# Values of two attentions computed token-major by their projections, instead of projected and then transposed

## The chip, the core and the metric

One core of a Trainium2 chip runs the whole program in one launch. The metric is the device time of that core in microseconds (us), the median of repeated runs. Nothing else runs on the chip.

## What is computed

Two transformer blocks run one after the other on 512 tokens of width 1024, in float32. The change lies in the first block, between its input norm and its attentions. Cut to that:

```python
h = rmsnorm(x, norm_mix_g)                       # (512, 1024)
q_a, k_a, v_a, q_b, k_b, v_b, gl_a, gl_b = jnp.split(h @ w_in, SPLITS, axis=-1)
# v_a: (512, 768), 12 heads of 64, in three groups of 4 with dilations 1, 4 and 16
# v_b: (512, 512), 8 heads of 64
o_a = dilated_attention(q_a, k_a, v_a)           # per group: softmax over every d-th key, probabilities @ v_a
o_b = stick_breaking_attention(q_b, k_b, v_b)    # probabilities @ v_b
merged = sigmoid(gl_a + b_a) * (o_a @ w_up_dil) + sigmoid(gl_b + b_b) * (o_b @ w_up_sb)
x = x + merged @ w_out
```

## The kernel before

**Products.** Activations lie feature-major: a tile holds 128 features on its partitions and the 512 tokens along it. A *slab* is 128 output features. For each slab TensorE (PE) takes the 8 tiles of 128 input features one after the other, loads a 128x128 block of the weight matrix as the stationary operand and streams the 512 tokens past it. Numbers are split into a high and a low part in the matmul's own format (`wh`, `wl` for weights, `Ah`, `Al` for activations), so that each product is three: high by high, high by low, low by high. A slab is therefore 8 x 3 = 24 matmuls 512 wide, into one PSUM bank; banks 0 and 1 alternate. This is `products`, called by `full_slab` (L2327 is the matmul in it).

**Weights.** Loads of 1 MB (256 columns of the matrix, all 1024 rows) go to `raw`, two slots; each serves two slabs. Per slab ScalarE (ACT) writes `wh` (L895) and VectorE (DVE) `wl` (L1439), both double-buffered. `lo_ready` counts them for PE.

**Order.** The slabs have numbers: 0 to 17 are q, k and v of the dilated attention (`T_QKV_A`), 18 to 25 the first gates, 26 to 37 q, k and v of the stick-breaking attention (`T_QKV_B`), 38 to 45 the second gates. The dilated attention itself is woven in behind slabs 18 to 29, the stick-breaking one behind slabs 38 and later. `slab_done` counts slabs that PE finished, `evac_done` slabs that DVE took out of PSUM; a slab starts when the one two before it is evacuated (`slab_start`).

**Values before.** Slabs 12 to 17 and 34 to 37 are values. The attentions need them token-major (tokens on the partitions), as the stationary operand of "probabilities times values". So each value slab is computed feature-major, evacuated by DVE into `vt` or `vtb` (L1915, L1484: times `RS`, the norm's reciprocal root of each token along the row), turned by PE in four 128x128 transposes (`v_turn`, L2578) into bank 6 or 7, and copied by ACT to `Vna` or `Vnb` (`v_copy`, L1180). For the heads with dilation 4 and 16 the evacuation writes the tokens sorted by their residue modulo 4 (`by_class`), so that the four transposes give one residue each:

```python
def by_class(ap):
    return ap.rearrange("p (c i) -> p i c", c=4)
```

**The start.** The input is turned to feature-major by PE (`turn_x`, L2494, four transposes for each of the 8 feature tiles), ACT takes out the high part (`x_hi`, L1149) and a plain copy (`x_copy`, L1145), DVE the low part (`x_lo`, L1846), and POOL and DVE split the first weights (L711, L1852). PE works on slabs 0 and 1 piece by piece as these arrive: `first_hh(k)`, `first_lh(k)` and `first_hl(k)` are the three products of feature tile k, each for both slabs (L2517). `warm(n)` (L2509) multiplies the identity by itself n times into a bank that nobody reads.

Of the kernel before, what the change touches and what calls it, by code (L numbers as in the profile page):

```python
# [171 lines left out]
def build(nc, d):  # L172
# [21 lines left out]
    with ctx:  # L194
# [59 lines left out]
        vt = region(13568, 2, 512)  # L254
# [9 lines left out]
        vtb = region(14080, 2, 512)  # L264
# [43 lines left out]
        r_x = stat[:, 4, 8:12]  # L308
# [24 lines left out]
        vtrans_done, vnat_copied = sem("vtrans_done"), sem("vnat_copied")  # L333
# [190 lines left out]

        def raw_slab(t):
            p, half, kt, n = slab[t]
            return raw_half(p % 2, half, kt, n)
# [76 lines left out]
        def _(sp):  # L604
# [50 lines left out]
            sp.wait_ge(vnat_copied, 6)  # L655
# [224 lines left out]
        def _(act):  # L880
# [280 lines left out]
            x_copy(5)  # L1161
            x_hi(6)
            x_hi(7)
            x_copy(7)
# [13 lines left out]
            def v_copy(i, dst):  # L1178
                act.wait_ge(vtrans_done, i + 1)
                act.activation(dst, ps[:, 6 + i % 2, :].rearrange("p (a b) -> p a b", a=4), ACT.Copy)\  # L1180
                   .then_inc(vnat_copied, 1)

            for t in range(T_QKV_A + 3, T_GATE_A):
                convert(t + 1)
                if t == T_QKV_A + 9:
                    act.wait_ge(vec_ready, 1)
                    act.activation(halfb[:, :], vecT[:, B_GATE:B_GATE + 16], ACT.Copy, scale=0.5)\
                       .then_inc(halfb_ready, 1)
                if t >= T_QKV_A + 14:
                    v_copy(t - 14, Vna[:, :, (t - 14) * P:(t - 13) * P])  # L1190
            v_copy(4, Vna[:, :, 4 * P:5 * P])
            convert(T_GATE_A + 1)
            v_copy(5, Vna[:, :, 5 * P:6 * P])
# [50 lines left out]
            for t in range(T_GATE_A + DIL_STEPS, T_GATE_B):  # L1244
                convert(t + 1)
                i = t - T_QKV_B - 8 - 2
                if i >= 0:
                    v_copy(6 + i, Vnb[:, :, i * P:(i + 1) * P])
            act.preload_act_table(ACT.Sigmoid)
            for i in (2, 3):  # L1250
                v_copy(6 + i, Vnb[:, :, i * P:(i + 1) * P])
# [176 lines left out]
        def _(dve):  # L1428
# [443 lines left out]
            def qkv_a(t, src):  # L1872

                i = t - T_QKV_A
                if i >= 14:
                    dve.wait_ge(vtrans_done, i - 13)
                dst = qa[:, i, :] if i < 6 else ka[:, i - 6, :] if i < 12 else vt[:, i % 2, :]
                if i < 6:
                    return by_block(dst), src.rearrange("p (n r c) -> p n r c", n=4, c=4)
                if i in (6, 7, 12, 13):  # L1880
                    return dst, src
# [29 lines left out]

            for t in range(T_QKV_A + 3, T_GATE_A + 1):
                dve.wait_ge(slab_done, t)
                dst, src = qkv_a(t - 1, dense_psum(t - 1, ONE))
                dve.tensor_tensor(dst, src, qkv_a(t - 1, RS[:, 0:S1])[1], ALU.mult).then_inc(evac_done, 1)  # L1915
# [38 lines left out]
            def qkv_b(t):  # L1954
                i = t - T_QKV_B
                if i == 0:
                    dve.wait_ge(scores_done, 8)
                if i >= 10:
                    dve.wait_ge(vtrans_done, 6 + i - 9)
                scaled(t, qb[:, i, :] if i < 4 else kb[:, i - 4, :] if i < 8 else vtb[:, i % 2, :], ONE)  # L1960
# [349 lines left out]
        def _(pe):  # L2310
# [20 lines left out]
            def slab_start(t):  # L2331
                pe.wait_ge(lo_ready, t + 1)
                if t >= 2:
                    pe.wait_ge(evac_done, t - 1)

# [207 lines left out]
            warm(4)  # L2543
            first_hh(0)
            first_hh(1)
            first_lh(0)
            turn_x(2)
            turn_x(3)
            first_lh(1)
            first_hl(0)  # L2550
# [66 lines left out]
            def dil_turn(u):  # L2617
                n, jp, nb, w, c1 = dil_unit(u)
                lg = Lg[u % 2]
                pe.wait_ge(p_norm, 2 * u + 2)  # L2620
                if u >= 1:
# [13 lines left out]
            def dil_pv(u):  # L2635
                n, jp, nb, w, c1 = dil_unit(u)
                pe.wait_ge(pt_copied, u + 1)
                if u == 0:
                    pe.wait_ge(vnat_copied, 6)
# [30 lines left out]
            for u in range(DIL_STEPS):  # L2670
                full_slab(T_GATE_A + u, Ah, Al, 0, ONE)
                if u == 0:
                    pe.wait_ge(evac_done, T_GATE_A)
                    v_turn(5, vt[:, 1, :])
# [8 lines left out]
            for t in range(T_GATE_A + DIL_STEPS, T_GATE_B):  # L2683
                full_slab(t, Ah, Al, 0, ONE)
                i = t - T_QKV_B - 9
                if i >= 0:
# [20 lines left out]
            def sb_turn(w):  # L2707
                n, hp, nk = sb_unit(w)
                pe.wait_ge(sb_probs, w + 1)
                if w >= 1:  # L2710
# [7 lines left out]
            def sb_pv_mm(w):  # L2718
                n, hp, nk = sb_unit(w)
                pe.wait_ge(sb_pt_copied, w + 1)  # L2720
                if w == 0:
                    pe.wait_ge(vnat_copied, 10)
# [10 lines left out]
            for i in range(SB_STEPS):  # L2733
                if i < 16:
# [6 lines left out]
                    if i == 0:  # L2741
                        pe.wait_ge(evac_done, T_GATE_B)
                        v_turn(9, vtb[:, 1, :])
# [198 lines left out]
```

## Time and profile before

| what | value |
|---|---|
| median of 3 runs | 1410.69 us (1410.23 to 1412.68) |
| the profiled execution | 1411.16 us, of which the span shown is 1409.4 us |
| granted TensorE clock, mean over the span | 0.999 |
| PE busy | 1402.3 us of the span, 8550 matmuls |
| DVE busy | 917.2 us |
| ACT busy | 592.8 us |
| POOL busy | 212.3 us |

The profile is of one execution; its time lies 0.5 us above the median. Busy time of PE counts overlapping matmuls once and their ends are modelled, so how long a stretch of matmuls really takes is read from the chain that ended last, which gives starts and counts.

### The profile page before, as it was taken

To read this page: it belongs to the slowest core of one execution; us is meant where nothing else is said; L and a number is where in the kernel's file an instruction comes from. 1 tells how busy PE (TensorE), PEld (TensorE's weight loads), DVE (VectorE), ACT (ScalarE), POOL (GpSimd) and SP (SyncE) were. 2 spreads that over 40 slices of the span, in tenths; PEclk is the share of its full clock that TensorE was granted. 3 is DMA by queue.
4 is the path that set the end of the run, shared out by engine and by line. 5 is a ranking of instruction groups with operands and counts; after the bars stand their busy time and mean duration, and the time that the engine had idled before them with its cause. 6 is when DMAs were issued, how large, how long until landed. Compare 5 with 4: busy or idle time off the path is not lost.

```text
span 1409.4 us, 21396 instructions
## 1 busy us (share of the span) xinstructions
PE 1402.3 (99%) x8550; PEld 1178.4 (84%) x8550; DVE 917.2 (65%) x1229; ACT 592.8 (42%) x844; POOL 212.3 (15%) x215
## 2 busy tenths in 40 slices
PE   9999999999999999999999999999999999999998
PEld 7887778777888989989888997778888998989886
DVE  6535433665757858677656677656756967758775
ACT  5124531554434435343244435344444535344353
POOL 5000000000022302211423020000022221302310
PEclk9999999999999999999999999999999999999999
DMA  5223113201227845736222322132225673937563
GB/s 183 90 90 113 61 60 96 84 31 60 90 90 179 181 125 152 169 106 162 90 90 85 110 61 84 60 105 90 90 90 135 178 166 109 215 93 184 144 174 110
DMA packets 154858, 161.58 MB, mean 115 GB/s; under 512 B 4010, under 2 KB 144660, under 8 KB 154788
## 3 DMA queue, kind: packets, MB, share of 16 engines
q1 hardware_dynamic: 122868, 129.12, 28.6%
q0 software_dynamic: 31904, 31.46, 12.3%
q8 instruction: 51, 0.84, 0.3%
q14 instruction: 19, 0.16, 0.0%
q10 hardware_dynamic: 16, 0.00, 0.0%
HBM read 157.68 MB, written 2.10 MB: 113 GB/s over the span
## 4 chain that ended last, share of the span: by engine, by line
PE 99%; DMA 0%; ACT 0%; DVE 0%; issue 0%; ACTq 0%
PE ps L2327 67%; PE ps L2374 17%; PE ps L2323 4%; PE ps L2447 3%; PE ps L2701 1%; PE ps L2517 1%; PE ps L2728 1%; PE ps L2714 1%; PE ps L2821 1%; PE ps L2605 0%; PE ps L2494 0%; PE ps L2578 0%; PE ps L2646 0%; PE ps L2625 0%; DMA arena<-in_x 0%; PE ps L2903 0%
## 5 line engine op out<-in xcount | busy, mean ns | idle before, releaser
L2327 PE MATMUL ps<-AA,wh 128*128 128x512 f32 x1600 | 504.2, 397 | 0.0
L2327 PEld LDWEIGHTS ps<-AA,wh 128*128 128x128 f32 x1600 | 297.0, 188 | 69.3 <-DVE wl L1439 0.8
L2327 PE MATMUL ps<-BB,wh 128*128 128x512 f32 x1088 | 342.2, 396 | 0.2 <-issue 0.2
L2327 PE MATMUL ps<-AA,wl 128*128 128x512 f32 x800 | 315.0, 394 | 0.0
L895 ACT ACTIVATE wh<-raw 128x1024 fp32r<-128x1024 f32 (+2 forms) x149 | 141.5, 950 | 253.7 <-PE ps L2327 243.8
L2327 PEld LDWEIGHTS ps<-BB,wh 128*128 128x128 f32 x1088 | 202.2, 188 | 49.3 <-issue 1.6
L2327 PE MATMUL ps<-BB,wl 128*128 128x512 f32 x544 | 214.0, 393 | 0.0
L1439 DVE TENSOR_TENSOR wl<-raw,wh 128x1024 fp32r<-128x1024 f32 (+2 forms) x149 | 169.9, 1140 | 47.8 <-ACT wh L895 47.5
L2327 PEld LDWEIGHTS ps<-AA,wl 128*128 128x128 f32 x800 | 150.5, 188 | 34.4
L2327 PEld LDWEIGHTS ps<-BB,wl 128*128 128x128 f32 x544 | 102.3, 188 | 23.3
L2374 PE MATMUL ps<-Hl,wh 128*128 128x256 f32 x384 | 108.0, 281 | 0.0
L1484 DVE TENSOR_TENSOR arena<-ps,RS 128x512 f32<-128x512 f32 (+2 forms) x59 | 40.7, 690 | 87.0 <-PE ps L2327 83.1
L1516 DVE TENSOR_TENSOR wl<-raw,wh 128x1024 fp32r<-128x1024 f32 x48 | 62.3, 1297 | 31.0 <-ACT wh L943 15.9
L2374 PE MATMUL ps<-Hl,Sh 128*128 128x256 f32 x288 | 81.1, 282 | 0.0
L2374 PEld LDWEIGHTS ps<-Hl,wh 128*128 128x128 f32 x384 | 72.3, 188 | 0.0
L943 ACT ACTIVATE wh<-raw 128x1024 fp32r<-128x1024 f32 x36 | 38.1, 1060 | 63.5 <-PE ps L2327 63.5
L1578 DVE SCALAR_TENSOR_TENSOR zf<-ps,RS 128x512 f32<-128x512 f32 x48 | 33.2, 692 | 45.2 <-PE ps L2327 44.4
L2374 PEld LDWEIGHTS ps<-Hl,Sh 128*128 128x128 f32 x288 | 54.2, 188 | 0.2
L2374 PE MATMUL ps<-AA,wh 128*128 128x256 f32 x192 | 54.3, 283 | 0.0
L2374 PE MATMUL ps<-BB,wh 128*128 128x256 f32 x192 | 54.0, 281 | 0.0
L2374 PE MATMUL ps<-AA,wl 128*128 128x256 f32 x192 | 53.8, 280 | 0.0
L2374 PE MATMUL ps<-BB,wl 128*128 128x256 f32 x192 | 53.8, 280 | 0.0
(397 smaller groups left out, 2231.2 us busy)
## 6 DMA issues: line engine op xcount, KB each, us to landing
raw<-in_w_in SPq DMA_DIRECT2D x38, 1024.0 KB, 5.2
raw<-in_w_ff SPq DMA_DIRECT2D x31, 1024.0 KB, 5.5
raw<-in_w_mlp_in SPq DMA_DIRECT2D x16, 1024.0 KB, 5.4
raw<-in_w_mlp_out SPq DMA_DIRECT2D x16, 1024.0 KB, 4.9
zf<-in_w_mlp_out POOLq DMA_DIRECT2D x48, 256.0 KB, 4.6
zf<-in_w_ff POOLq DMA_DIRECT2D x48, 256.0 KB, 4.8
raw<-in_w_out SPq DMA_DIRECT2D x8, 1024.0 KB, 4.9
arena<-in_x SPq DMA_DIRECT2D x4, 512.0 KB, 6.9
```

The costliest lines, as they stand in the source:

```text
L895: act.activation(w_slab(wh, t % 2, kt), raw_slab(t), ACT.Copy).then_inc(hi_ready, 1)
L943: act.activation(w_slab(wh, j % 2, KT), raw_half((p0 + i) % 2, j % 2, KT, 2), ACT.Copy)\
L1439: dve.tensor_tensor(w_slab(wl, t % 2, kt), raw_slab(t), w_slab(wh, t % 2, kt), ALU.subtract)\
L1484: dve.tensor_tensor(tokens(dst, kind), dense_psum(t, kind)[0:rows], tokens(scale, kind), ALU.mult)\
L1516: dve.tensor_tensor(w_slab(wl, slot, KT), raw_half(p % 2, slot, KT, 2), w_slab(wh, slot, KT), ALU.subtract).then_inc(lo_ready, 1)
L1578: dve.scalar_tensor_tensor(out=f, in0=halves(dense_psum(t0 + j, which)), scalar=0.0, in1=halves(RS[:, 0:S1]), op0=ALU.max, op1=ALU.mult).t ...
L2323: last = pe.matmul(dense_psum(t_ps, ALL)[:, half, :], a[:, k, :], b[:, o0 + k, half * HALF2:(half + 1) * HALF2], start=start, stop=stop)
L2327: last = pe.matmul(dense_psum(t_ps, kind), a[:, k, :], b[:, o0 + k, col0:col0 + S1], start=start, stop=stop)
L2374: mm = pe.matmul(ps[:, bank, 0:HB], w[:, k, :], hidden_part(x, k, b), start=(first and k == 0 and i == 0), stop=(k == 3 and i == 2), skip_ ...
L2447: mm = pe.matmul(ps[:, bank, :], x, v[:, k, :], start=(first and k == 0 and n == 0), stop=(k == 3 and n == 2), skip_group_check=True)
L2517: return pe.matmul(dense_psum(t, ONE), w_slab(w, t, KT)[:, k, :], x[:, k, 0:S1], start=first, stop=last)
L2701: pe.matmul(ps[:, 2 + b, 0:nk], qb[rows, hp, n * P:(n + 1) * P], kb[rows, hp, 0:nk], start=True, stop=False)
```

## The change

Value slabs are computed in pairs, token-major. The stationary operand becomes a 128x128 block of the activations (128 features by 128 tokens), the moving one a block of the weights, 128 features by 256 output columns, which is two slabs at once. Both halves of a pair keep their slab number: the first takes input tiles 0 to 3, the second tiles 4 to 7 (`value_unit`), each 4 x 4 x 3 = 48 matmuls 256 wide, into two banks of 4 to 7 that hold 4 token blocks by 256 columns. For the heads with dilation 4 and 16 (slabs 14 to 17) the stationary block is every fourth column of `Ah` or `Al`, so that the residues come out sorted. DVE evacuates a pair in four TENSOR_SCALARs of 256 columns, times the reciprocal root of the token, which now lies on the partition (`r_x`; for sorted tokens `r_class`, got by four transposes of `RS` into bank 6 and a copy of four columns). `vt`, `vtb`, `v_turn`, `v_copy` and their semaphores go; the waits that stood on `vnat_copied` now stand on `evac_done`. At the start `warm(4)` goes, `first_hl(0)` moves ahead of the turns of tiles 2 and 3, and ACT does `x_copy(5)` behind `x_hi(7)`.

```diff
@@ -522,8 +520,25 @@
             r, c = (CHUNKS - 1) * DM + (0 if upper else S1), 0 if left else S1
             return w[r:r + S1, c:c + S1]
 
+        T_V_A, T_V_B = T_QKV_A + 12, T_QKV_B + 8
+        V_ENDS = {T_V_A: T_GATE_A, T_V_B: T_GATE_B}
+
+        def value_start(t):
+
+            return next((v for v, end in V_ENDS.items() if v <= t < end), None)
+
+        def value_banks(t):
+
+            return 4 + 2 * ((t - value_start(t)) // 2 % 2)
+
+        def value_blocks(w, t):
+
+            return w[:, t % 2, :].rearrange("p (k n) -> p k n", k=4)
+
         def raw_slab(t):
             p, half, kt, n = slab[t]
+            if value_start(t) is not None:
+                return raw[:, p % 2, half * DM:(half + 1) * DM].rearrange("p (k n) -> p k n", k=KT)
             return raw_half(p % 2, half, kt, n)
 
         def lr_slab(col):
...
@@ -1158,9 +1173,9 @@
             x_hi(5)
             x_copy(3)
             x_copy(4)
-            x_copy(5)
             x_hi(6)
             x_hi(7)
+            x_copy(5)
             x_copy(7)
             for a in range(4):
                 if a == 1:
...
@@ -1175,22 +1190,13 @@
             act.activation(r_x, r_x, ACT.Sqrt).then_inc(sqrt_ready, 1)
 
 
-            def v_copy(i, dst):
-                act.wait_ge(vtrans_done, i + 1)
-                act.activation(dst, ps[:, 6 + i % 2, :].rearrange("p (a b) -> p a b", a=4), ACT.Copy)\
-                   .then_inc(vnat_copied, 1)
-
             for t in range(T_QKV_A + 3, T_GATE_A):
                 convert(t + 1)
                 if t == T_QKV_A + 9:
                     act.wait_ge(vec_ready, 1)
                     act.activation(halfb[:, :], vecT[:, B_GATE:B_GATE + 16], ACT.Copy, scale=0.5)\
                        .then_inc(halfb_ready, 1)
-                if t >= T_QKV_A + 14:
-                    v_copy(t - 14, Vna[:, :, (t - 14) * P:(t - 13) * P])
-            v_copy(4, Vna[:, :, 4 * P:5 * P])
             convert(T_GATE_A + 1)
-            v_copy(5, Vna[:, :, 5 * P:6 * P])
 
             act.wait_ge(halfb_ready, 1)
 
...
@@ -1909,10 +1908,27 @@
                 q, r = qkv_a(t, RS[:, 0:S1])
                 dve.tensor_tensor(q, q, r, ALU.mult).then_inc(late_scaled, 1)
 
+            def value_rows(dst, t, r):
+                dve.wait_ge(slab_done, t + 1)
+                at = (t - value_start(t)) // 2 * 256
+                for a in range(4):
+                    mul = dve.tensor_scalar(dst[:, a, at:at + 256],
+                                            ps[:, value_banks(t) + a // 2, a % 2 * 256:a % 2 * 256 + 256],
+                                            r[:, a:a + 1], None, ALU.mult)
+                    if a % 2:
+                        mul.then_inc(evac_done, 1)
+
             for t in range(T_QKV_A + 3, T_GATE_A + 1):
-                dve.wait_ge(slab_done, t)
-                dst, src = qkv_a(t - 1, dense_psum(t - 1, ONE))
-                dve.tensor_tensor(dst, src, qkv_a(t - 1, RS[:, 0:S1])[1], ALU.mult).then_inc(evac_done, 1)
+                if t - 1 < T_V_A:
+                    dve.wait_ge(slab_done, t)
+                    dst, src = qkv_a(t - 1, dense_psum(t - 1, ONE))
+                    dve.tensor_tensor(dst, src, qkv_a(t - 1, RS[:, 0:S1])[1], ALU.mult).then_inc(evac_done, 1)
+                elif (t - 1 - T_V_A) % 2:
+                    value_rows(Vna, t - 1, r_x if t - 1 < T_V_A + 2 else r_class)
+                if t == T_V_A:
+                    dve.wait_ge(r_turned, 1)
+                    dve.tensor_copy(r_class, ps[:, 6, 0:S1:P]).then_inc(r_class_ready, 1)
+                    dve.wait_ge(r_class_ready, 1)
                 if t < T_GATE_A:
                     convert(t + 1)
                 if t in (T_QKV_A + 4, T_QKV_A + 5):
...
@@ -2330,8 +2347,26 @@
 
             def slab_start(t):
                 pe.wait_ge(lo_ready, t + 1)
-                if t >= 2:
+                if t in (T_GATE_A, T_GATE_A + 1):
+                    pe.wait_ge(evac_done, T_V_A)
+                elif t in (T_GATE_B, T_GATE_B + 1):
+                    pe.wait_ge(evac_done, T_V_B)
+                elif t >= 2:
                     pe.wait_ge(evac_done, t - 1)
+
+            def value_unit(t, by_residue):
+                pe.wait_ge(lo_ready, t + 1)
+                half = (t - value_start(t)) % 2
+                h, l = value_blocks(wh, t), value_blocks(wl, t)
+                for k in range(4):
+                    for a in range(4):
+                        of = slice(a, S1, 4) if by_residue else slice(a * P, (a + 1) * P)
+                        xh, xl = Ah[:, 4 * half + k, of], Al[:, 4 * half + k, of]
+                        for i, (x, w) in enumerate(((xh, h), (xh, l), (xl, h))):
+                            mm = pe.matmul(ps[:, value_banks(t) + a // 2, a % 2 * 256:a % 2 * 256 + 256], x, w[:, k, :],
+                                           start=(half == 0 and k == 0 and i == 0 and a % 2 == 0),
+                                           stop=(half == 1 and k == 3 and i == 2), skip_group_check=True)
+                mm.then_inc(slab_done, 1)
 
             def full_slab(t, Oh, Ol, o0, kind, ready=None, col0=0):
                 kt = slab[t][2]
...
@@ -2540,14 +2575,13 @@
 
             turn_x(0)
             turn_x(1)
-            warm(4)
             first_hh(0)
             first_hh(1)
             first_lh(0)
+            first_hl(0)
             turn_x(2)
             turn_x(3)
             first_lh(1)
-            first_hl(0)
             first_hl(1)
             first_hh(2)
             turn_x(4)
...
@@ -2570,14 +2604,6 @@
                 mm.then_inc(slab_done, 1)
 
 
-            def v_turn(i, src):
-
-                if i >= 2:
-                    pe.wait_ge(vnat_copied, i - 1)
-                for a in range(4):
-                    mm = pe.transpose(ps[:, 6 + i % 2, a * P:(a + 1) * P], src[:, a * P:(a + 1) * P], ident[:, :])
-                mm.then_inc(vtrans_done, 1)
-
             for t in range(2, T_GATE_A):
                 if t == 3:
                     def first_stats():
...
@@ -2585,15 +2611,23 @@
                         pe.wait_ge(xt_copied_act, len(X_ON_ACT))
                         stats(0)
                     slab_with_stats(t, (Ah, Al), ONE, None, first_stats, 2)
+                elif t < T_V_A:
+                    full_slab(t, Ah, Al, 0, ONE)
                 else:
-                    full_slab(t, Ah, Al, 0, ONE)
+                    if t == T_V_A:
+                        pe.wait_ge(meta_copied, 1)
+                    if t == T_V_A + 2:
+                        pe.wait_ge(r_class_ready, 1)
+                    if t == T_V_A + 4:
+                        pe.wait_ge(evac_done, T_V_A + 2)
+                    value_unit(t, t >= T_V_A + 2)
                 if t == 3:
                     turn_vectors()
-                if t >= 13:
-                    pe.wait_ge(evac_done, t)
-                    if t == 13:
-                        pe.wait_ge(x_diag, 5)
-                    v_turn(t - 13, vt[:, (t - 1) % 2, :])
+                if t == T_V_A - 2:
+                    pe.wait_ge(x_diag, 5)
+                    for c in range(4):
+                        mm = pe.transpose(ps[:, 6, c * P:(c + 1) * P], RS[:, c:S1:4], ident[:, :])
+                    mm.then_inc(r_turned, 1)
 
 
             def dil_scores(u):
...
@@ -2681,13 +2714,14 @@
 
 
             for t in range(T_GATE_A + DIL_STEPS, T_GATE_B):
-                full_slab(t, Ah, Al, 0, ONE)
-                i = t - T_QKV_B - 9
-                if i >= 0:
-                    pe.wait_ge(evac_done, t)
-                    if i == 0:
-                        pe.wait_ge(oa_ready, 4)
-                    v_turn(6 + i, vtb[:, i % 2, :])
+                if t < T_V_B:
+                    full_slab(t, Ah, Al, 0, ONE)
+                    continue
+                if t == T_V_B:
+                    pe.wait_ge(pt_copied, 8)
+                if t == T_V_B + 2:
+                    pe.wait_ge(oa_ready, 4)
+                value_unit(t, False)
 
 
             def sb_scores_mm(w):
```

How it moves instructions, at the places that the prediction speaks of. First PE at the start of the program, before (L2494 turns `xnat`, the input as it lies in memory, in `arena`; L2509 is `warm`, L2517 the pieces of slabs 0 and 1):

```order
4 L2494 MATMUL ps<-ident,arena 128x128 [waits x_in0]
5 L2494 MATMUL ps<-ident,arena 128x128 x3
6 L2494 MATMUL ps<-ident,arena 128x128 [waits x_in0]
7 L2494 MATMUL ps<-ident,arena 128x128 x3
8 L2509 MATMUL ps<-ident 128x128 x4
9 L2517 MATMUL ps<-AA,wh 128x512 [waits hi_split,w_first_hi]
10 L2517 MATMUL ps<-AA,wh 128x512
11 L2517 MATMUL ps<-AA,wh 128x512 [waits hi_split,w_first_hi]
12 L2517 MATMUL ps<-AA,wh 128x512
13 L2517 MATMUL ps<-AA,wh 128x512 [waits act_ready]
14 L2517 MATMUL ps<-AA,wh 128x512
15 L2494 MATMUL ps<-ident,arena 128x128 [waits x_in1]
```

and now:

```order
4 L2529 MATMUL ps<-ident,arena 128x128 [waits x_in0]
5 L2529 MATMUL ps<-ident,arena 128x128 x3
6 L2529 MATMUL ps<-ident,arena 128x128 [waits x_in0]
7 L2529 MATMUL ps<-ident,arena 128x128 x3
8 L2552 MATMUL ps<-AA,wh 128x512 [waits hi_split,w_first_hi]
9 L2552 MATMUL ps<-AA,wh 128x512
10 L2552 MATMUL ps<-AA,wh 128x512 [waits hi_split,w_first_hi]
11 L2552 MATMUL ps<-AA,wh 128x512
12 L2552 MATMUL ps<-AA,wh 128x512 [waits act_ready]
13 L2552 MATMUL ps<-AA,wh 128x512
14 L2552 MATMUL ps<-AA,wl 128x512 [waits w_first_lo]
15 L2552 MATMUL ps<-AA,wl 128x512
```

The four matmuls of `warm` are gone, and two products with `wl` stand ahead of the turns that wait for `x_in1`.

Then DVE from slab 11's evacuation on, before (`arena<-ps,RS 128x512` are evacuations, `wl<-raw,wh` the low weights of the next slab):

```order
59 L1915 TENSOR_TENSOR arena<-ps,RS 128x128x4 [waits slab_done]
60 L1439 TENSOR_TENSOR wl<-raw,wh 128x1024 [waits hi_ready]
61 L1915 TENSOR_TENSOR arena<-ps,RS 128x512 [waits slab_done]
62 L1439 TENSOR_TENSOR wl<-raw,wh 128x1024 [waits hi_ready]
63 L1915 TENSOR_TENSOR arena<-ps,RS 128x512 [waits slab_done]
64 L1439 TENSOR_TENSOR wl<-raw,wh 128x1024 [waits hi_ready]
65 L1915 TENSOR_TENSOR arena<-ps,RS 128x128x4 [waits vtrans_done,slab_done]
66 L1439 TENSOR_TENSOR wl<-raw,wh 128x1024 [waits hi_ready]
67 L1915 TENSOR_TENSOR arena<-ps,RS 128x128x4 [waits vtrans_done,slab_done]
68 L1439 TENSOR_TENSOR wl<-raw,wh 128x1024 [waits hi_ready]
69 L1915 TENSOR_TENSOR arena<-ps,RS 128x128x4 [waits vtrans_done,slab_done]
```

and now:

```order
59 L1925 TENSOR_TENSOR arena<-ps,RS 128x128x4 [waits slab_done]
60 L1930 COPY stat<-ps 128x4 [waits r_turned]
61 L1440 TENSOR_TENSOR wl<-raw,wh 128x1024 [waits hi_ready,r_class_ready]
62 L1440 TENSOR_TENSOR wl<-raw,wh 128x1024 [waits hi_ready]
63 L1915 TENSOR_SCALAR arena<-ps,stat 128x256 [waits slab_done]
64 L1915 TENSOR_SCALAR arena<-ps,stat 128x256 x3
65 L1440 TENSOR_TENSOR wl<-raw,wh 128x1024 [waits hi_ready] x2
66 L1915 TENSOR_SCALAR arena<-ps,stat 128x256 [waits slab_done]
67 L1915 TENSOR_SCALAR arena<-ps,stat 128x256 x3
68 L1440 TENSOR_TENSOR wl<-raw,wh 128x1024 [waits hi_ready] x2
69 L1915 TENSOR_SCALAR arena<-ps,stat 128x256 [waits slab_done]
```

Six evacuations of one slab each became three groups of four TENSOR_SCALARs 256 wide, one group for each second slab, and the wait on `vtrans_done` went with the transposes; one copy of four columns that waits for `r_turned` came in.

## Rows read from the trace of the kernel before

**Rows 1.** The page: span, PE's busy time, granted clock in 40 slices, last chain.

```profile
span 1409.4 us, 21396 instructions
...
PE 1402.3 (99%) x8550; PEld 1178.4 (84%) x8550; DVE 917.2 (65%) x1229; ACT 592.8 (42%) x844; POOL 212.3 (15%) x215
...
PEclk9999999999999999999999999999999999999999
...
PE 99%; DMA 0%; ACT 0%; DVE 0%; issue 0%; ACTq 0%
```

**Rows 2.** Chain that ended last, 90 to 140 us: start us, us, engine and line, instructions.

```profile
90.31 0.44 PE ps L2578 x4
90.75 5.58 PE ps L2327 x24
96.33 0.44 PE ps L2578 x4
...
114.85 5.59 PE ps L2327 x24
120.44 0.44 PE ps L2578 x4
```

**Rows 3.** The same chain, 420 to 560 us, products 256 wide.

```profile
461.66 39.92 PE ps L2374 x336
```

**Rows 4.** The same chain, 758 to 842 us, products 264 wide.

```profile
789.72 17.59 PE ps L2323 x144
```

**Rows 5.** Timeline of DVE, 84 to 100 us: a value evacuation of each layout.

```profile
84.78 0.69 DVE L1915 TENSOR_TENSOR arena<-ps,RS 128x512 f32<-128x512 f32 x1 [3.24 <-PE ps L2327]
90.35 0.69 DVE L1915 TENSOR_TENSOR arena<-ps,RS 128x512 f32<-128x512 f32 x1 [3.19 <-PE ps L2327]
96.37 1.11 DVE L1915 TENSOR_TENSOR arena<-ps,RS 128x512 f32<-128x512 f32 x1 [3.70 <-PE ps L2327]
```

**Rows 6.** Groups of ACT by line and form: busy us, mean ns, idle before.

```profile
L895 ACT ACTIVATE wh<-raw 128x256 fp32r<-128x256 f32 x8 | 3.3, 417 | 9.1 <-PE ps L2327 9.1
L1227 ACT ACTIVATE BB<-ps 128x256 fp32r<-128x256 f32 x4 | 2.4, 609 | 0.0
```

**Rows 7.** The last chain, 0 to 45 us.

```profile
4.88 1.97 PE ps L2494 x8
6.85 1.30 PE ps L2509 x8
8.15 1.38 PE ps L2517 x6
9.52 0.87 PE ps L2494 x8
10.40 1.86 PE ps L2517 x8
...
21.99 7.22 PE ps L2327 x30
```

**Rows 8.** Timeline of ACT, 0 to 30 us.

```profile
6.10 1.48 ACT L1149 ACTIVATE AA<-ps,vecT 128x512 fp32r<-128x512 f32 x2 [3.35 <-PE ps L2494]
...
15.92 1.27 ACT L1149 ACTIVATE AA<-ps,vecT 128x512 fp32r<-128x512 f32 x2 [0.43 <-PE ps L2494]
18.10 0.60 ACT L1145 ACTIVATE X<-ps 128x512 f32<-128x512 f32 x1 [0.91 <-DVE AA L1846]
18.59 1.05 ACT L1172 ACTIVATE SQ<-arena 128x1024 f32<-128x1024 f32 x1
...
19.63 1.05 ACT L895 ACTIVATE wh<-raw 128x1024 fp32r<-128x1024 f32 x1
```

**Rows 9.** Timeline of DVE, 0 to 30 us.

```profile
7.56 0.68 DVE L1852 TENSOR_TENSOR wl<-raw,wh 128x512 fp32r<-128x512 f32 x1
...
20.71 1.23 DVE L1439 TENSOR_TENSOR wl<-raw,wh 128x1024 fp32r<-128x1024 f32 x1 [0.36 <-ACT wh L895]
```

**Rows 10.** Timeline of PE's weight loads, 0 to 30 us.

```profile
21.99 0.30 PEld L2327 LDWEIGHTS ps<-AA,wh 128*128 128x128 f32 x2 [0.46 <-DVE wl L1439]
```

More of the change, by code:

```diff
@@ L253, in build @@
         PT = region(13568, 2, 512)
-        vt = region(13568, 2, 512)
         GA = region(15104, 8, 512)
@@ L263, in build @@
         PTb = region(14080, 2, 512)
-        vtb = region(14080, 2, 512)
         xnat = region(15104, 4, 1024)
@@ L307, in build @@
         y_sum, y_eps, r_tok = stat[:, 0, 0:8], stat[:, 1, 0:4], stat[:, 4, 0:4]
-        r_x = stat[:, 4, 8:12]
+        r_x, r_class = stat[:, 4, 8:12], stat[:, 4, 12:16]
         params_in, gain_in = sem("params_in"), sem("gain_in")
@@ L332, in build @@
             sem("xt_psum"), sem("xt_copied"), sem("meta_psum"), sem("meta_copied"))
-        vtrans_done, vnat_copied = sem("vtrans_done"), sem("vnat_copied")
+        r_turned, r_class_ready = sem("r_turned"), sem("r_class_ready")
         gate_done = sem("gate_done")
@@ L654, in _ @@
                 load(p)
-            sp.wait_ge(vnat_copied, 6)
+            sp.wait_ge(evac_done, T_GATE_A)
             for n in range(2):
@@ L1245, in _ @@
                 convert(t + 1)
-                i = t - T_QKV_B - 8 - 2
-                if i >= 0:
-                    v_copy(6 + i, Vnb[:, :, i * P:(i + 1) * P])
             act.preload_act_table(ACT.Sigmoid)
-            for i in (2, 3):
-                v_copy(6 + i, Vnb[:, :, i * P:(i + 1) * P])
             def sb_sigmoids(w):
@@ L1874, in qkv_a @@
                 i = t - T_QKV_A
-                if i >= 14:
-                    dve.wait_ge(vtrans_done, i - 13)
-                dst = qa[:, i, :] if i < 6 else ka[:, i - 6, :] if i < 12 else vt[:, i % 2, :]
+                dst = qa[:, i, :] if i < 6 else ka[:, i - 6, :]
                 if i < 6:
                     return by_block(dst), src.rearrange("p (n r c) -> p n r c", n=4, c=4)
-                if i in (6, 7, 12, 13):
+                if i in (6, 7):
                     return dst, src
@@ L1957, in qkv_b @@
                     dve.wait_ge(scores_done, 8)
-                if i >= 10:
-                    dve.wait_ge(vtrans_done, 6 + i - 9)
-                scaled(t, qb[:, i, :] if i < 4 else kb[:, i - 4, :] if i < 8 else vtb[:, i % 2, :], ONE)
+                if i < 8:
+                    scaled(t, qb[:, i, :] if i < 4 else kb[:, i - 4, :], ONE)
+                elif i % 2:
+                    value_rows(Vnb, t, r_x)
             for u in range(DIL_STEPS):
@@ L2620, in dil_turn @@
                 pe.wait_ge(p_norm, 2 * u + 2)
+                if u == 0:
+                    pe.wait_ge(evac_done, T_GATE_A)
                 if u >= 1:
@@ L2638, in dil_pv @@
                 if u == 0:
-                    pe.wait_ge(vnat_copied, 6)
+                    pe.wait_ge(evac_done, T_GATE_A)
                 k = u // 2
@@ L2671, in _ @@
                 full_slab(T_GATE_A + u, Ah, Al, 0, ONE)
-                if u == 0:
-                    pe.wait_ge(evac_done, T_GATE_A)
-                    v_turn(5, vt[:, 1, :])
                 if 0 <= u - 3 < 8:
@@ L2683, in _ @@
             for t in range(T_GATE_A + DIL_STEPS, T_GATE_B):
-                full_slab(t, Ah, Al, 0, ONE)
-                i = t - T_QKV_B - 9
-                if i >= 0:
-                    pe.wait_ge(evac_done, t)
-                    if i == 0:
-                        pe.wait_ge(oa_ready, 4)
-                    v_turn(6 + i, vtb[:, i % 2, :])
+                if t < T_V_B:
[6 more added lines that the diff above has]
+                value_unit(t, False)
             def sb_scores_mm(w):
@@ L2709, in sb_turn @@
                 pe.wait_ge(sb_probs, w + 1)
+                if w == 0:
+                    pe.wait_ge(evac_done, T_GATE_B)
                 if w >= 1:
@@ L2721, in sb_pv_mm @@
                 if w == 0:
-                    pe.wait_ge(vnat_copied, 10)
+                    pe.wait_ge(evac_done, T_GATE_B)
                 if hp == 0 and w >= 8:
@@ L2740, in _ @@
                         mm.then_inc(slab_done, 1)
-                    if i == 0:
-                        pe.wait_ge(evac_done, T_GATE_B)
-                        v_turn(9, vtb[:, 1, :])
                 else:
```

## The prediction

> **What bounds the kernel now.** I read the page first. PE is busy 99% of a span of 1409.4 us, the chain that ended last lies on PE for 99% of it, and the granted clock stands at full speed in all 40 slices [rows 1]. So time is what PE's queue takes, matmul by matmul. The other engines only matter where PE waits for them, and it does so almost nowhere: the one clear wait near the change is 0.46 us before slab 2 [rows 10]. Next I read the chain in order of time around the value slabs. It shows slab (5.58 to 5.59 us for 24 matmuls, 233 ns each), turn (0.44 us for four transposes, 110 ns each), slab, turn, without a hole [rows 2]. The edit is thus priced by PE's rate for 256-wide matmuls, which I take from another stage that runs them, and by how fast PE loads a stationary operand that is read at a step of four elements, which no row shows. The start of the program is a case of its own, read from its chain and the timelines of ACT and DVE [rows 7 to 10].
>
> **The change part by part.**
>
> *Products.* Ten value slabs of 24 matmuls at 5.58 us are 55.8 us [rows 2]. They become five pairs of 96 matmuls 256 wide, 480 in all. In the MLP, 336 matmuls 256 wide take 39.92 us, 118.8 ns each [rows 3]. 264 wide, 144 take 17.59 us, 122.2 ns [rows 4]. The difference of 3.3 ns for 8 columns is streaming at full clock, so at 256 columns the streaming sets the rate and the load of the next stationary block is hidden, as long as it is no slower than now. 480 x 118.8 ns = 57.0 us: **+1.2 us**. The arithmetic is the same, but half as wide a matmul pays its fixed 12 ns (118.8 less the 106.7 that 256 columns take at 2.4 GHz) twice as often.
>
> *Turns.* Ten groups of four transposes go, 10 x 0.44 = **-4.4 us** [rows 2]. All of it is on the chain. Four transposes of the token scale come in behind slab 10, at 110 ns each: **+0.4 us**. They wait for the scale in `RS`, which slab 3's evacuation already uses, so they wait for nothing.
>
> *Evacuations.* DVE did 0.69 us a slab for the plain layout and 1.11 us for the sorted one, and was then idle over 3 us before the next [rows 5]. Four TENSOR_SCALARs of 256 columns per pair should take between 1.1 us (two plain slabs less a little) and 1.7 us (ACT's 417 ns for a 256-wide copy, four times [rows 6]), so they fit in that idle time, and with them the small copy of the residue scale ahead of slab 13's weights: **0**. If the cover were gone, each pair would cost up to 1.7 us. PE does not stand behind them: the next pair writes two other banks, and the gates use banks 0 and 1. The ten copies on ACT go, off the chain: 0. SP's transfer of the sorted values waits for the last pair's evacuation, one copy less than before: 0. The load order of the weights is unchanged.
>
> *The start.* `warm(4)` takes 1.30 us of the chain [rows 7]. What it covered: the high part of tile 0 is ready when ACT's first two are done, halfway from 6.10 to 7.58 us [rows 8], that is at about 6.84 us, where the turns end (4.88 + 1.97 [rows 7]). So PE can begin the products at once. But eight turns take 1.97 us there and 0.87 us later [rows 7], though the profile shows the clock granted: whatever slows PE that early would also slow the first two products, which now stand there, by at most their own 0.47 us. The second tile's high part is ready at 7.58, the low weights at 8.24 us [rows 8, 9], just when `first_hl(0)` wants them. I book 1.30 - 0.4 = 0.9 us. For it to reach the end, slab 2 must begin earlier too. It waits for DVE's low weights (begun 20.71, 1.23 us long), these for ACT's high ones (19.63), these stand behind a square (18.59) and a copy (18.10) that waited 0.91 us for DVE's low part of tile 7 [rows 8 to 10]. That chain begins at the turns of tiles 6 and 7, after which ACT works at 15.92 [rows 8]; they move up with PE, and the 0.60 us copy that ACT now does later would else have been in the way. So the whole chain moves: **-0.9 us**, between 0 (ACT, DVE or the input's arrival holds the old time) and -1.3.
>
> *The stationary operand at a step of four.* For slabs 14 to 17 (192 of the 480 matmuls) PE loads every fourth column of `Ah` or `Al`, float32, one element in each 16 bytes. Every load before is of neighbouring columns. The lower bound is nothing. For the upper I take what engines here pay per element for such a step: ACT 609 ns for 256 elements written at a step of four against 417 ns [rows 6], 0.75 ns each; DVE 1.11 against 0.69 us for 512 [rows 5], 0.82 ns each. For 128 columns that is 96 to 105 ns more per load. There is nearly no room to hide it: a transpose is a load of 128 columns and a stream of 128, and its 110 ns [rows 2] is twice what the stream needs, so a load takes up to 110 of the 118.8 ns. Loads would then set the rate at 206 to 215 ns, 87 to 96 ns more than 118.8, and 192 of them cost 16.7 to 18.4 us. I take **0**. Both rows of the penalty are about writes; the nearest row for a read is the load itself, which takes one column in some 0.83 ns, slower than PE streams its moving operand (0.42 ns), so the memory has shown it can serve twice the rate of a load. That is an argument, not a row, so the upper end stays in the range.
>
> Here the Trainium skill speaks against the change: Advanced Engine Details and Errata, section Memory Cachelines, says that an access needs at least two hits on a 16-byte line of SBUF, and that a different line for each access costs performance. A step of four float32 is a new line each time. It gives no figure, and no row before shows it on a load of PE.
>
> The sum: +1.2 - 4.4 + 0.4 - 0.9 = -3.7 us. Against the profiled execution, 1411.16 us (the span of 1409.4 and 1.8 us around it), this gives 1407.5. That execution stands 0.5 us over the median, so against 1410.69 the forecast is **1407.0 us**, 0.26% less. A change of 0.2% or 2.8 us is about what a measurement of this kernel can tell from none.
>
> **The rivals.**
>
> *Strided loads set the rate (slower).* Place: slabs 14 to 17. Price: +16.7 to +18.4 us on top of -3.7, so 1423.7 to 1425.4 us. It decides from about 20 ns per load: 192 x 19 = 3.7 us eats the gain. For it: ACT's and DVE's rows, and that a load has hardly 10 ns of room. Against it: those are writes, and PE's stream shows that reads run at twice the load's rate. By the skill's line rule this is what happens.
>
> *The gain is smaller than what can be told.* The start gives nothing, since ACT, DVE or the arrival of the input holds slab 2 at 21.99 us, or the 256-wide matmuls run a few ns slower than in the MLP. Each alone: -3.7 + 0.9 = -2.8, 1407.9; or 480 x 3 ns = +1.4, 1408.4. Both: 1409.3. For it: the 0.46 us wait shows that DVE already holds slab 2 now. Against: that DVE work hangs on PE's own turns.
>
> *A turn cost more than its 0.44 us.* If leaving them also saves a switch of 0.1 us each, 1406.0.
>
> **How the numbers follow.** Forecast with its neighbours down to 1405.5 and up to 1407.8: 0.51. A gain too small to tell, 1407.9 to 1409.5: 0.17. Strided loads: 0.32, most of it at 1423.7 to 1425.4, some of it a smaller penalty in between. The time I give is that of the likeliest case, whose own range is 1405.5 to 1409.5. To hold 8 in 10 the range must reach into the strided case: 1405.5 to 1425.0. Chances: faster by over 0.2% 0.51, within 0.17, slower 0.32.
>
> **What would show it.** In the changed profile's chain: value slabs of 48 matmuls at 5.7 us each, the same for slabs 12, 13 and 34 to 37 (neighbouring columns) as for 14 to 17 (step of four). If the latter take 9.9 to 10.3 us and weight loads start 206 to 215 ns apart, the strided rival holds. Slab 2 should begin at about 21.1 instead of 21.99 us; if it begins there as before, the start gave nothing. DVE should show groups of four TENSOR_SCALARs that end well before PE's next need, and no wait of PE on them. I am wrong in kind if PE waits at the first unit that uses banks 4 to 7 again, or at the transposes behind slab 10.

## The result, and the profile after

The changed kernel takes 1430.45 us (1430.04 to 1431.92, 4 runs) against 1411.04 us: a ratio of 1.0139, 95% interval 1.0126 to 1.0152. It is 19.4 us slower. The forecast was 1407.0 us in a range of 1405.5 to 1425.0; the time lies outside it.

The page of the changed kernel, the lines that answer to [rows 1]:

```profile
span 1428.5 us, 21772 instructions
...
PE 1421.1 (99%) x8746; PEld 1207.5 (85%) x8746; DVE 916.8 (64%) x1240; ACT 588.0 (41%) x834; POOL 211.7 (15%) x215
...
PEclk9999999999999999999999999999999999999999
...
PE 99%; ACT 0%; DVE 0%; issue 0%; POOL 0%; POOLq 0%; DVEq 0%; ACTq 0%
```

These lines don't tell what happened: PE is still 99% busy at a granted clock of 0.999, and the chain still lies on PE. The page's groups give a first sign, the loads of `value_unit` (L2366) beside those of an unchanged stage:

```profile
L2409 PEld LDWEIGHTS ps<-Hl,wh 128*128 128x128 f32 x384 | 72.4, 189 | 0.0
L2366 PEld LDWEIGHTS ps<-wh,AA 128*128 128x128 f32 x320 | 65.9, 246 | 0.1
```

One of `value_unit` is shown as 246 ns long on average against 189. The time itself is read from the chain that ended last. Its pieces from the start of slab 2 to the second gates (L2366 is the matmul of `value_unit`, L2344 that of `products`, L2629 the four transposes of the residue scale, L2552 the products of slabs 0 and 1):

```profile
15.40 5.64 PE ps L2552 x24
21.03 0.04 issue
21.08 7.23 PE ps L2344 x30
...
72.73 0.47 PE ps L2629 x4
73.20 5.56 PE ps L2344 x24
78.76 56.49 PE ps L2366 x288
135.25 5.58 PE ps L2344 x24
```
```profile
250.93 22.74 PE ps L2366 x192
273.67 2.80 PE ps L2344 x12
```

Slabs 34 to 37 are 192 matmuls in 22.74 us, 118.4 ns each, as forecast. Slabs 12 to 17 are 288 in 56.49 us. Slabs 12 and 13 load neighbouring columns like those; at their rate they are 96 x 118.4 ns = 11.4 us of it, which leaves 45.1 us for slabs 14 to 17: **235 ns for each of 192 matmuls**. DVE's evacuations, one behind each pair of slabs, show the same split:

```profile
90.17 1.66 DVE L1915 TENSOR_SCALAR arena<-ps,stat 128x256 f32<-128x256 f32 x4 [3.31 <-PE ps L2366]
...
112.73 1.66 DVE L1915 TENSOR_SCALAR arena<-ps,stat 128x256 f32<-128x256 f32 x4 [8.90 <-PE ps L2366]
...
135.29 1.66 DVE L1915 TENSOR_SCALAR arena<-ps,stat 128x256 f32<-128x256 f32 x4 [8.90 <-PE ps L2366]
```

The first pair ends 11.4 us behind the chain's 78.76 us, the other two take 22.56 us each, 235 ns for each of 96 matmuls. Weight loads, in a stretch of slab 12 or 13 and in one of slabs 14 to 17:

```profile
85.36 0.19 PEld L2366 LDWEIGHTS ps<-wl,AA 128*128 128x128 f32 x1
85.48 0.31 PEld L2366 LDWEIGHTS ps<-wh,AA 128*128 128x128 f32 x2
85.72 0.19 PEld L2366 LDWEIGHTS ps<-wl,AA 128*128 128x128 f32 x1
```
```profile
104.16 0.33 PEld L2366 LDWEIGHTS ps<-wl,AA 128*128 128x128 f32 x1
104.39 0.57 PEld L2366 LDWEIGHTS ps<-wh,AA 128*128 128x128 f32 x2
104.86 0.33 PEld L2366 LDWEIGHTS ps<-wl,AA 128*128 128x128 f32 x1
105.10 0.57 PEld L2366 LDWEIGHTS ps<-wh,AA 128*128 128x128 f32 x2
```

A load of neighbouring columns is shown as 0.19 us long, and one begins each 0.12 us (three in the 0.36 us from 85.36 to 85.72). A load at the step of four is shown as 0.33 us long, and one begins each 0.23 us (three in the 0.70 us from 104.16 to 104.86). That this load sets PE's pace is tested below.

What the change moved, on the chain, before and after:

| part | us |
|---|---|
| start: slab 2 begins at 21.08 instead of 21.99 | -0.9 |
| four transposes of the residue scale | +0.5 |
| 10 groups of transposes | -4.4 |
| 480 matmuls at 118.4 ns instead of 240 at 232 to 233 | +1.0 |
| 192 loads at the step of four, 235 - 118.4 ns each | +22.4 |
| sum | +18.6 |
| difference of the two spans | +19.1 |

The last 0.5 us comes up behind the value slabs, where both kernels run the same code: from there on the two chains are 18.5 to 19.0 us apart, up and down, and 19.0 at the end. No run tells what it is; executions of one kernel differ by more than that (1407.44 to 1409.95 us for the first experiment below).

### The profile page after: what moved, and what is told of

The parts are those of the page before. It is cut to its first block, busy times and chain, and to the rows that moved or that the text cites. A ratio compares the mean times of both kernels' runs of the same rounds, so it can differ in the third digit from the quotient of the medians.

```text
span 1428.5 us, 21772 instructions
## 1 busy us (share of the span) xinstructions
PE 1421.1 (99%) x8746; PEld 1207.5 (85%) x8746; DVE 916.8 (64%) x1240; ACT 588.0 (41%) x834; POOL 211.7 (15%) x215
## 4 chain that ended last, share of the span: by engine, by line
PE 99%; ACT 0%; DVE 0%; issue 0%; POOL 0%; POOLq 0%; DVEq 0%; ACTq 0%
PE ps L2344 62%; PE ps L2409 17%; PE ps L2366 6%; PE ps L2340 4%; PE ps L2482 3%; PE ps L2735 1%; PE ps L2552 1%; PE ps L2764 1%; PE ps L2750 1%; PE ps L2854 1%; PE ps L2639 0%; PE ps L2682 0%; PE ps L2661 0%; PE ps L2936 0%; PE ps L2529 0%; PE ps L2700 0%
## 5 line engine op out<-in xcount | busy, mean ns | idle before, releaser
L2344 PE MATMUL ps<-AA,wh 128*128 128x512 f32 x1440 | 453.5, 396 | 0.2
L2344 PE MATMUL ps<-BB,wh 128*128 128x512 f32 x1088 | 342.2, 396 | 0.2 <-issue 0.2
L2344 PEld LDWEIGHTS ps<-AA,wh 128*128 128x128 f32 x1440 | 267.4, 188 | 62.8 <-DVE wl L1440 1.0
L2344 PE MATMUL ps<-AA,wl 128*128 128x512 f32 x720 | 283.4, 394 | 0.0
L2344 PEld LDWEIGHTS ps<-BB,wh 128*128 128x128 f32 x1088 | 202.1, 188 | 49.2 <-issue 1.4
L2344 PE MATMUL ps<-BB,wl 128*128 128x512 f32 x544 | 213.9, 393 | 0.0
L2344 PEld LDWEIGHTS ps<-AA,wl 128*128 128x128 f32 x720 | 135.4, 188 | 30.9
L2344 PEld LDWEIGHTS ps<-BB,wl 128*128 128x128 f32 x544 | 102.3, 188 | 23.4
L2366 PE MATMUL ps<-wh,AA 128*128 128x256 f32 x320 | 75.0, 328 | 0.0
L2366 PEld LDWEIGHTS ps<-wh,AA 128*128 128x128 f32 x320 | 65.9, 246 | 0.1
```

The source lines that it names most:

```text
L2344: last = pe.matmul(dense_psum(t_ps, kind), a[:, k, :], b[:, o0 + k, col0:col0 + S1], start=start, stop=stop)
L2366: mm = pe.matmul(ps[:, value_banks(t) + a // 2, a % 2 * 256:a % 2 * 256 + 256], x, w[:, k, :], start=(half == 0 and k == 0 and i == 0 and ...
```

## The experiments

Theory S, formed on the result: the step of the stationary operand (the distance between the columns that one load reads) sets the rate in slabs 14 to 17. Its rivals are that something else about these four slabs does it (the residue scale, the banks, the evacuations), or that the step slows PE whatever it streams.

### Neighbouring columns in slabs 14 to 17

```diff
-                        of = slice(a, S1, 4) if by_residue else slice(a * P, (a + 1) * P)
+                        of = slice(a * P, (a + 1) * P)
```

> The changed kernel, but slabs 14 to 17 load neighbouring columns of the activations (a block of 128 tokens) instead of every fourth, so the values of the heads with dilation 4 and 16 come out unsorted; nothing else moves. Theory S (the step of the stationary operand sets the rate): slabs 14 to 17 fall from 235 ns a matmul to the 118.4 ns that slabs 34 to 37 show, 192 x 116.5 ns = 22.4 us less, so about 1408.0 us against 1430.45. Rival P (the place does it: the scale r_class, the banks, or the evacuations around slabs 14 to 17): the stretch stays at 56.5 us and the time near 1430.

1408.3 us (1407.44 to 1409.95, 10 runs) against 1411.09: ratio 0.9981, interval 0.9972 to 0.9991. The chain:

```profile
79.59 34.11 PE ps L2366 x288
113.70 5.58 PE ps L2344 x24
```

34.11 us for the same 288 matmuls, 118.4 ns each. The step is the whole loss, and theory S holds: all other work of the slabs (scale, banks, evacuations) was still there. What is left of the change gives 2.8 us (1.3 to 4.0 by the interval).

### Steps of two, three and eight

The question was what the load pays for. The edit replaces the slice above, for the four slabs:

```diff
+ slice(a // 2 * 256 + a % 2, a // 2 * 256 + 256, 2)    # step 2
+ slice(a, a + 3 * (P - 1) + 1, 3)                      # step 3
+ y.rearrange("p k n -> p (k n)")[:, at:at + 8 * (P - 1) + 1:8]    # step 8, at = min(kt, 6) * S2 + a
```

> The changed kernel, but slabs 14 to 17 load every second column (8 bytes apart, two in each 16 bytes) instead of every fourth; values come out in a wrong order. Theory L (a line of 16 bytes is read once for its columns, two per line are enough): 118 to 119 ns a matmul, about 1408 us. Theory N (any step but one halves the load): 235 ns, 1430 us. Between them, a load that pays by the bytes it spans: 118 ns too, since 2 x 128 x 4 bytes would be half of what 235 ns cover.

> The changed kernel, but slabs 14 to 17 load every third column (12 bytes apart; three of four columns begin a new 16-byte line); values come out of wrong tokens. Theory L, each new line costs 235/128 = 1.84 ns and nothing else counts: 0.75 lines a column, 176 ns a load and a matmul, 192 x (176 - 118.4) = +11.1 us over the 1408.3 of the run with neighbours, about 1419.4 us. Theory T (two columns of each line or the full price, no step between): 118 or 235 ns, 1408 or 1430 us.

> The changed kernel, but slabs 14 to 17 load every eighth column of the activations laid end to end (32 bytes apart, a line of its own for each and one line skipped between two); values wrong. One small memset at the start clears the 16 unused columns of each tile. Theory L (each new line costs 1.84 ns, lines passed over cost nothing): 235 ns a matmul as at step 4, 1430.5 us. Rival B (the load pays by the bytes that it spans): 470 ns, 192 x 235 = +45 us, 1475 us.

Measured 1407.34, 1419.45 and 1431.14 us, one run each. The chains, in this order:

```profile
78.42 34.46 PE ps L2366 x288
```
```profile
79.27 45.13 PE ps L2366 x288
```
```profile
78.71 57.77 PE ps L2371 x288
```

Taking off 96 x 118.44 ns = 11.37 us for slabs 12 and 13 and dividing by 192:

| step, columns | new 16-byte lines per column | ns a matmul | ns a new line (128 columns) |
|---|---|---|---|
| 1 | 0.25 | 118.4 | stream sets the rate |
| 2 | 0.5 | 120.3 | stream sets the rate |
| 3 | 0.75 | 175.8 | 1.83 |
| 4 | 1 | 235 | 1.84 |
| 8 | 1 | 241.7 | 1.89 |

A *line* is here an aligned piece of 16 bytes, four float32 columns. These loads pay for each new line that they touch, 1.84 ns, and hardly for lines that they pass over: the rival that pays by the bytes spanned wanted 470 ns at step 8 and falls. The size of 16 bytes comes out of the same table: pieces of 8 bytes would make step 3 as dear as step 4, pieces of 32 would make step 8 twice as dear as step 4. At step 2 the load would be 118 ns by this price and just fits under the stream. Step 3 was forecast at 176 ns and 1419.4 us before it ran. Theory N (any step but one costs the full price) falls with step 2, theory T (two columns of each line or the full price) with step 3. The 6.7 ns between steps 4 and 8 stay unexplained. The price is not that of every load: the four transposes of `RS` don't pay it (last section).

The Trainium skill's rule that the prediction set against the change (Advanced Engine Details and Errata, Memory Cachelines: two hits on a 16-byte line, a penalty where each access has a line of its own) is borne out by these loads: two hits, step 2, cost 1.9 ns a matmul; one hit, step 4, took 235 instead of 118.4 ns.

### The step under a stream of 512 columns

```diff
-                            last = pe.matmul(dense_psum(t_ps, kind), a[:, k, :], b[:, o0 + k, col0:col0 + S1],
+                            aw = a[:, k, :]
+                            if kind == ONE and 12 <= t_ps < 18:
+                                at = k // 4 * S1 + k % 4
+                                aw = (wl if i == 2 else wh)[:, slot, at:at + 4 * (P - 1) + 1:4]
+                            last = pe.matmul(dense_psum(t_ps, kind), aw, b[:, o0 + k, col0:col0 + S1],
```

> The kernel before, but slabs 12 to 17 read their stationary weights at a step of four columns (of wrong columns, so these values are wrong), each load under a stream of 512 columns. If a load at a step of four takes some 235 ns and runs beside the stream of the matmul before it, a slab goes from 5.58 us to at most 24 x 235 = 5.64 us, +0.4 us for the six, 1411.4 us. If the step stalls PE itself, each matmul pays 116 ns more whatever it streams: 144 x 116 ns = 16.7 us, 1427.7 us.

1411.29 us, one run, against 1411.09. Its chain (L2331 is `products` there) and its weight loads:

```profile
90.85 5.78 PE ps L2331 x24
103.29 5.78 PE ps L2331 x24
...
115.73 5.58 PE ps L2331 x24
```
```profile
84.83 0.31 PEld L2331 LDWEIGHTS ps<-AA,wl 128*128 128x128 f32 x1
85.06 0.54 PEld L2331 LDWEIGHTS ps<-AA,wh 128*128 128x128 f32 x2
85.53 0.31 PEld L2331 LDWEIGHTS ps<-AA,wl 128*128 128x128 f32 x1
```

The loads are shown as 0.31 us long, nearly as in the changed kernel, and three of them still begin in 0.70 us; but that is also what streams of 512 columns take. A slab goes from 5.58 (the last row is a gate slab, unchanged) to 5.78 us, 241 instead of 233 ns a matmul. So the step does not add its 116 ns whatever is streamed: the load runs beside the matmul ahead of it. At most 5.64 us a slab was expected, for a load of 235 ns; some 6 ns a matmul more than the load is longer than the stream stay unexplained. The price in the changed kernel comes from two edits together, the step and the halving of the stream to 256 columns.

### The start alone

```diff
             turn_x(1)
-            warm(4)
             first_hh(0)
             first_hh(1)
             first_lh(0)
+            first_hl(0)
             turn_x(2)
             turn_x(3)
             first_lh(1)
-            first_hl(0)
...
             x_copy(4)
-            x_copy(5)
             x_hi(6)
             x_hi(7)
+            x_copy(5)
```

> The kernel before with only the start of the change: no warm(4), first_hl(0) ahead of the turns of tiles 2 and 3, x_copy(5) behind x_hi(7). Forecast: slab 2 begins at 21.1 us instead of 21.99 and the rest is moved by as much, -0.9 us, about 1410.1 us. Rival: the head start is lost at a later wait of the first block, 1411.0 us.

1410.57 us (1410.05 to 1412.01, 10 runs) against 1411.09; ratio 0.9998, interval 0.9988 to 1.0007. The timing can't tell 0.5 us from nothing. The chain of this kernel, and below it that of the kernel with step 3, which has the same start:

```profile
4.79 1.90 PE ps L2494 x8
6.69 0.08 issue
6.77 2.41 PE ps L2517 x8
9.18 0.87 PE ps L2494 x8
...
15.52 5.64 PE ps L2517 x24
21.16 0.02 issue
21.18 7.22 PE ps L2327 x30
```
```profile
1.85 7.22 DMA arena<-in_x
9.11 1.09 PE ps L2529 x8
...
15.85 5.70 PE ps L2552 x24
21.57 7.24 PE ps L2344 x30
```

The forecast mechanism is there: the first products begin at 6.77 us, 0.08 us behind the turns, and slab 2 at 21.18. But in the nine profiles with this start slab 2 began at 20.73 to 21.90 us (21.08 in the changed kernel, 21.90 with neighbouring columns), against 21.99 us in the kernel before. The chain with step 3 tells why it can be late: there the turns of tiles 2 and 3 wait until 9.07 us for the input (1.85 + 7.22). In the kernel before they begin at 9.52 us [rows 7], behind the four warm matmuls, so an input that comes at 9.07 us would hold up nothing there. The head start at slab 2 is thus 0.1 to 1.3 us, and the input's arrival is a part of that spread; what else is in it no run separates.

### Versions that keep the order of the residues

The first repair follows from the run under 512 columns. Slabs 12 and 13 stay a pair; slabs 14 to 17 and 34 to 37 become groups of four, each number taking 2 tiles of the contraction and streaming 512 columns. The pair's sums go to banks 2 and 3, those of a group to banks 4 to 7, and the waits on evacuations move accordingly. Cut to the main lines, with comments put in:

```diff
+    def quad(base):
+        for j in range(2):
+            add("quad", (j, base), KT, 2)      # a load is 512 rows by 512 columns
...
-                        xh, xl = Ah[:, 4 * half + k, of], Al[:, 4 * half + k, of]
+                        xh, xl = Ah[:, tiles * part + k, of], Al[:, tiles * part + k, of]
...
-                            mm = pe.matmul(ps[:, value_banks(t) + a // 2, a % 2 * 256:a % 2 * 256 + 256], x, w[:, k, :],
+                            mm = pe.matmul(value_out(t, a), x, w[:, k, :],     # ps[:, 4 + a, :] in a group of four
```

> A version that keeps the order of the residues. Slabs 12 and 13 stay a pair; slabs 14 to 17, and 34 to 37, become groups of four: a load brings 512 rows by 512 columns of the weights, each slab number takes 2 tiles of the contraction, the stream is 512 wide and each of 4 token blocks has a bank of 4 to 7. The loads at a step of four are kept but stand under streams of 512. By the run with strided weights under 512 columns, such a slab takes about 24 x 240 = 5.8 us and the others 5.58. Sum on before: turns -4.4, residue scale +0.4, pair +0.2, four strided slabs +0.7, start -0.5 to -0.9: -3.6 to -4.0, 1407.1 to 1407.5 us against 1411.1. If the strided load is not hidden under the activations' stream as it was under the weights', 96 x 116 ns = 11 us more, 1418 us.

1407.46 us (1406.37 to 1408.04, 7 runs) against 1411.17: ratio 0.9973, interval 0.9962 to 0.9984. Beside it ran the same version with neighbouring columns:

> The version with groups of four, but slabs 14 to 17 load neighbouring columns, so that the values of the heads with dilation 4 and 16 come out unsorted: what the step still costs under 512 columns. Expected slabs of 5.58 us instead of 5.8, 0.7 us less than with the step.

1406.84 us, one run. The stretch of slabs 12 to 17 in the first and the second, then slabs 34 to 37, which are alike in both (L2385 is `value_unit`):

```profile
79.11 34.27 PE ps L2385 x192
```
```profile
78.66 33.55 PE ps L2385 x192
```
```profile
229.06 22.16 PE ps L2385 x96
```

34.27 against 33.55 us: under 512 columns the step of four costs 96 x 7.5 ns = 0.7 us, where it cost 22.4. That is again more than a load of 235 ns under a stream of 231 would cost.

The other repair takes the step off PE. ACT writes sorted copies of the activations, two tiles behind each of slabs 4 to 11:

```diff
+                    for X_, Y_ in ((Ah, Bh), (Al, Bl)):
+                        act.activation(Y_[:, t - T_QKV_A - 4, 0:S1].rearrange("p (c i) -> p c i", c=4),
+                                       X_[:, t - T_QKV_A - 4, 0:S1].rearrange("p (i c) -> p c i", c=4),
+                                       ACT.Copy).then_inc(sorted_ready, 1)
```

> The version with groups of four, in which ACT, idle most of that stretch, copies Ah and Al sorted by residue into the space of Bh and Bl, which nobody uses until the dilated attention's output, two tiles of 512 columns behind each of slabs 4 to 11; slabs 14 to 17 load neighbouring columns of the copies. 16 copies of 0.63 us (if the read at a step of four costs ACT nothing) to 1.1 us each lie in ACT's idle time of over 3 us per slab. Slabs 14 to 17 should take 5.58 instead of 5.76 us: 0.7 us less than the version that loads at the step, 1406.8 us; the same as that version if the copies delay ACT's weights.

1406.56 us (1406.12 to 1407.47, 7 runs) against 1410.68: ratio 0.9971, interval 0.9960 to 0.9982. Chain, and ACT's groups from 30 to 85 us:

```profile
78.85 33.55 PE ps L2396 x192
```
```profile
L1221 ACT ACTIVATE BB<-AA 128x512 fp32r<-128x512 f32 x16 | 17.2, 1123 | 0.0
L930 ACT ACTIVATE wh<-raw 128x1024 fp32r<-128x1024 f32 x10 | 10.6, 1063 | 30.4 <-PE ps L2371 25.7 <-PE ps L2396 4.7
```

The 17.2 us of copies lie in ACT's idle time and the stretch is 33.55 us. Both versions are faster than both kernels, by 0.27 and 0.29% of the kernel before; their intervals don't tell them apart, the chain puts the copies 0.7 us ahead.

## Why the prediction was wrong

*What bounds the kernel.* Right: PE's queue is the time, before and after.

*Products.* Right. 118.8 ns a matmul was read from the MLP [rows 3], 118.4 measured; the term is +1.0 instead of +1.2 us.

*Turns.* Right: -4.4 us, and +0.47 instead of +0.4 for the residue scale. PE never waited for it.

*Evacuations.* Right in that they cost nothing. DVE in the changed kernel, behind slab 11:

```profile
78.80 1.11 DVE L1925 TENSOR_TENSOR arena<-ps,RS 128x512 f32<-128x512 f32 x1 [3.65 <-PE ps L2344]
79.75 0.17 DVE L1930 COPY stat<-ps 128x4 f32<-128x4 f32 x1
```

Behind a pair, four TENSOR_SCALARs take 1.66 us, the upper end of what was given, after at least 3.31 us of idle time. The lower end, 1.1 us for "two plain slabs less a little", was not what the rows give: two plain slabs are 1.38 us.

*The start.* The mechanism was right. That the changed kernel's profile has -0.91 us, the very number forecast, is luck: the other eight profiles have -0.1 to -1.3. The input's arrival was named only as a reason for no gain at all; the chains show it taking a part, as far as the warm matmuls no longer cover it. By the timing of the start alone the gain can't be told from none. The rest of the forecast, without the step, was 3.7 us less; the run with neighbouring columns shows 2.8, with slab 2 at 21.90 us in its profile.

*The step of four.* This is the step that failed. The text gave bounds of 0 and 16.7 to 18.4 us and took 0; the runs show +22.4 us. The reason given was that PE's stream reads a column in 0.42 ns and a load needs one only each 0.83 ns, so that "the memory has shown it can serve twice the rate of a load". That counted columns where, by the runs with steps 3, 4 and 8, lines count. The stream reads four neighbouring columns of each line: 0.42 ns a column is 1.67 ns a line. To stay hidden at the step of four, a load needs a new line each 0.93 ns (118.8 ns for 128), and no row had shown that. So the stream's rate was no ground for 0. Had it been taken as the limit for lines, the estimate would have been 128 x 1.67 = 214 ns a load and 18.3 us. That 1.67 ns lies near the measured 1.84 is not shown to have one cause with it: the transposes of `RS` load faster than either (last section). The other argument, that both rows of a penalty were writes, was no evidence for reads being free; ACT's copies in the last version supply a row for a read at a step of four: 1123 ns for 512 columns.

*The rivals.* The one that came true was named, with its place and with 0.32. Its price was 4 to 6 us too low: the rows gave 0.75 and 0.82 ns more per element on top of a load of 110 ns, together 206 to 215 ns, and it was 235. Most of the 5.4 us by which the time lies past the range's end is that. The price was borrowed from two other engines, and the 0.82 ns is not even of a step of four: DVE's evacuation `by_class` writes at a step of 128 columns (`p (c i) -> p i c`). The rule of the Trainium skill that the prediction named (Advanced Engine Details and Errata, Memory Cachelines) had no figure, but it speaks of any access, and does not set reads apart as the argument for 0 did.

## What to carry to other kernels

Count what the stationary operand of a product touches in lines of 16 bytes, not in columns: at 1.84 ns for each new line, as measured on `Ah` and `Al`, a load at a step of four takes 235 ns against a stream of 256 columns that takes 118; under one of 512 it costs 8 ns. When an edit both narrows the stream and makes the load longer, price the load against the new stream. If tokens must come out sorted, let an idle engine sort them once, or keep the stream wide.

When bounds lie far apart, say in which unit a row supports the lower one. Here the stream's rate was read per column; per line it did not reach what a hidden load needs.

## What was not expected of the hardware

The price of a load is linear in new lines between steps 3 and 4 (175.8 and 235 ns), with nothing visible at step 2, where it hides under the stream. The four transposes of `RS`, whose loads also read every fourth column, hardly showed it: 0.47 us against 0.44 for neighbouring columns; their loads are shown as 197 to 212 ns long, against 140 for the value transposes before. In the changed kernel:

```profile
72.33 0.68 PEld L2629 LDWEIGHTS ps<-ident,RS 128*128 128x128 f32 x4
72.92 0.31 PEld L2344 LDWEIGHTS ps<-AA,wh 128*128 128x128 f32 x2
```

At 1.84 ns a line the four would take 0.94 us; the next slab's load begins 0.59 us behind the first of them, so a line took at most 1.15 ns. The price measured in slabs 14 to 17 is therefore not that of every load. These four differ in being transposes and in their operand, which is plain float32 and not in the matmul's own format; which of the two matters was not tried, and it rests on four instructions. ACT pays for a read at a step of four what it pays for such a write or more: 1123 ns for 512 elements of the copies, where a copy of 512 neighbouring columns takes 632, so 0.96 ns more per element, against 0.75 in [rows 6]. The group of ACT in the kernel before that gives the 632 ns:

```profile
L985 ACT ACTIVATE AA<-zf 128x512 fp32r<-128x512 f32 x12 | 7.6, 632 | 12.7 <-DVE zf L1590 12.7
```
